# Norm statistics with tokens on partitions: root and reciprocal over 128x4 elements, spread to a bank by TensorE

## The reference

```python
def _rms_norm(x, g):
    xf = x.astype(jnp.float32)
    y = xf * lax.rsqrt(jnp.mean(xf * xf, axis=-1, keepdims=True) + NORM_EPS)
    return (y * g.astype(jnp.float32)).astype(x.dtype)

x = x + _diff_attention(_rms_norm(x, a_norm_g[j]), ...)   # blocks 0 and 3
x = x + _conformer_conv(_rms_norm(x, b_norm_g[j]), ...)   # block 1
x = x + _mla(_rms_norm(x, c_norm_g[j]), ...)              # block 2
# second network, per layer:
h = rmsnorm(x, norm1_g[layer]) * (1 + scale) + shift
x = x + g1 * mixer_or_attention(h)
x = x + g2 * swiglu(rmsnorm(x, norm2_g[layer]) * (1 + scale2) + shift2, w_gu, w_down)
```

## Time and profile before

| | us |
|---|---|
| median of 3 runs | 3501.59 (3496.18 to 3503.17) |
| profiled execution, its own time | 3498.49 |
| its span | 3496.7 |
| TensorE busy, matmuls | 3179.1 (91%) |
| TensorE busy, weight loads | 2494.1 (71%) |
| VectorE busy | 1874.4 (54%) |
| ScalarE busy | 1124.6 (32%) |
| GpSimd busy | 112.7 (3%) |

### The profile page before, as it was taken

The page is one execution under the profiler, slowest core; times in us unless marked ns, Lnnn a source line. Parts: engine busy times, 40 slices in busy tenths (PEclk is TensorE's granted clock), DMA queues, the critical chain, the costliest instruction groups (busy, mean ns, idle before and its releaser), DMA issues. The chain is left out here.

```text
span 3496.7 us, 39262 instructions
## 1 busy us (share of the span) xinstructions
PE 3179.1 (91%) x15464; PEld 2494.1 (71%) x15464; DVE 1874.4 (54%) x2778; ACT 1124.6 (32%) x2065; POOL 112.7 (3%) x114
## 2 busy tenths in 40 slices
PE   6998897899889988988999897799999989989997
PEld 4876564666668753478888566688888867767875
DVE  4648698844765677634234698524333355442333
ACT  3346323344342632232122222321211144532221
POOL 0000000100100000001000021000000000000000
PEclk9999999899999999999999998999999999999999
DMA  4224211321322241221111225312222111122221
GB/s 147 85 61 157 90 50 62 129 72 37 134 101 91 73 165 80 89 80 48 62 61 36 95 73 207 130 60 97 84 77 78 51 57 30 66 73 95 96 89 56
DMA packets 57151, 299.18 MB, mean 86 GB/s; under 512 B 8375, under 2 KB 8631, under 8 KB 31080
## 3 DMA queue, kind: packets, MB, share of 16 engines
q1 hardware_dynamic: 52504, 280.87, 22.7%
q0 software_dynamic: 4496, 16.26, 1.5%
HBM read 269.05 MB, written 15.73 MB: 81 GB/s over the span
## 5 line engine op out<-in xcount | busy, mean ns | idle before, releaser
L410 PE MATMUL bank<-high,slot_high 128*128 128x512 f32 (+1 forms) x3344 | 1236.3, 370 | 122.5 <-DVE low L334 77.8
L411 PE MATMUL bank<-low,slot_high 128*128 128x512 f32 (+1 forms) x3344 | 1226.0, 367 | 0.0
L412 PE MATMUL bank<-high,slot_low 128*128 128x512 f32 (+1 forms) x3344 | 1222.1, 365 | 0.0
L390 DVE TENSOR_TENSOR slot_low<-slot,slot_high 128x2048 fp32r<-128x2048 f32 (+1 forms) x172 | 390.3, 2270 | 1053.9 <-ACT slot_high L384 1053.8
L410 PEld LDWEIGHTS bank<-high,slot_high 128*128 128x128 f32 x3344 | 633.8, 190 | 261.1 <-issue 118.2
L384 ACT ACTIVATE slot_high<-slot 128x2048 fp32r<-128x2048 f32 (+1 forms) x172 | 325.5, 1893 | 1354.0 <-PE bank L412 1161.4
L411 PEld LDWEIGHTS bank<-low,slot_high 128*128 128x128 f32 x3344 | 635.5, 190 | 109.1 <-issue 4.6
L412 PEld LDWEIGHTS bank<-high,slot_low 128*128 128x128 f32 x3344 | 633.8, 190 | 108.0
L1089 DVE TENSOR_REDUCE least<-bank 128x1 f32<-128x128 f32 (+2 forms) x224 | 105.2, 504 | 131.5 <-PE bank L3402 51.7
L1140 ACT ACTIVATE prob<-bank,least 128x128 f32<-128x128 f32 (+2 forms) x224 | 121.2, 555 | 36.8 <-DVE least L1093 29.8
L449 PE MATMUL bank<-slot_high,low 128*128 128x256 f32 x448 | 125.7, 280 | 0.0
(11 more groups left out here) (381 smaller groups left out, 3778.0 us busy)
## 6 DMA issues: line engine op xcount, KB each, us to landing
slot<-in_gu SPq DMA_DIRECT2D x44, 1024.0 KB, 4.8
slot<-in_a_in SPq DMA_DIRECT2D x32, 1024.0 KB, 4.9
mod_raw<-in_mod SPq DMA_DIRECT2D x44, 512.0 KB, 4.7
slot<-in_e_rest SPq DMA_DIRECT2D x16, 1024.0 KB, 4.8
slot<-in_down SPq DMA_DIRECT2D x16, 1024.0 KB, 4.7
a_value<-in_mod SPq DMA_DIRECT2D x24, 512.0 KB, 3.4
spectra<-f_spectrum SPq DMA_DIRECT2D x12, 1024.0 KB, 3.8
h_spectrum<-spectra SPq DMA_DIRECT2D x12, 1024.0 KB, 5.0
```

Source lines behind the costliest of these rows:

```text
L390: dve.tensor_tensor(k.slot_low[s][:, 0:n], k.slot[s][:, 0:n], k.slot_high[s][:, 0:n].bitcast(F32), ALU.subtract).then_inc(k.low[s], 1)
L410: pe.matmul(out, wh, xh, start=kt == 0, stop=False)
L411: pe.matmul(out, wh, xl, start=False, stop=False)
L412: mm = pe.matmul(out, wl, xh, start=False, stop=kt == self.kt - 1)
```

## The change

The means come out with tokens on partitions. The squares are now the stationary operand, 128 tokens at a time, and a single column of the mean matrix is the moving one: four fp32 matmuls per 512 tokens and k tile, each with one column, and the bank holds 128x4 elements. ScalarE reads the bank and takes the root of mean plus 1e-6 (a bias column `eps`), VectorE the reciprocal, both over 128x4 (128x2 for context). TensorE then spreads it: with the column of 128 tokens broadcast as stationary operand and the identity as moving operand, four matmuls fill the bank with the reciprocals, repeated on all partitions. The feed's `make` reads the bank, and the bank is given back when all tiles are made. `take_means` and the 512-wide root and reciprocal remain for `Statistics` alone.

Beside it: a dummy root (`warm_root`) runs ahead of the squares, both in the norms that sum their own and in `TailSquares`; the feed makes two tiles ahead in the place of three, in all feeds; the second weight split always follows the feed; and in `project_a` VectorE runs the norm before it waits for the lambda vectors. The core of the diff:

```diff
 class Core:
+        self.token_root, self.token_rstd = (self.sb(n, TOK // P) for n in ("token_root", "token_rstd"))
+        self.warm, self.warmed = self.sb("warm", 16), 0
...
+    def warm_root(self, act):
+        act.activation(self.warm[:, self.warmed:self.warmed + 1], self.c("eps", 1), ACT.Sqrt)
+        self.warmed += 1
...
 class Feed:
-        for y in range(3):
+        for y in range(2):
             build(y)
...
-            build(y + 3)
+            build(y + 2)
...
 class SplitNorm:
     def make(self, y, dst):
+        rstd = self.k.rstd[:, c:c + n] if self.given else self.k.ps[7 - r][:, 0:n]
         return self.dve.scalar_tensor_tensor(dst, self.k.X[:, kt * TOK + c:kt * TOK + c + n], self.gain(r, kt),
-                                             self.k.rstd[:, c:c + n], ALU.mult, ALU.mult)
+                                             rstd, ALU.mult, ALU.mult)
...
     def square(self, k, act):
+        k.warm_root(act)
...
     def take_roots(self, k, act, u):
         for r, (c, n) in enumerate(self.ranges):
+            act.wait_ge(k.filled[7 - r], self.full(u, r))
+            act.activation(k.token_root[:, self.token_columns(r)], k.ps[7 - r][:, 0:n // P], ACT.Sqrt,
+                           bias=k.c("eps", 1)).then_inc(root.sem, 1)
...
     def tensor(self, k, pe, u):
+        if not self.summed:
...
+                mm = sum_tokens(k, pe, k.ps[7 - r], self.operand.ring[y % 4][:, 0:self.ranges[r][1]], kt == 0, kt == KT - 1)
...
+        for r, (c, n) in enumerate(self.ranges):
+            pe.wait_ge(inverse.sem, inverse.at(r + 1))
+            for j in range(n // P):
+                one = k.token_rstd[:, 4 * r + j:4 * r + j + 1]
+                mm = pe.matmul(k.ps[7 - r][:, j * P:(j + 1) * P], one.broadcast_to([P, P]), k.c("ident"),
+                               start=True, stop=True)
+            mm.then_inc(wide.sem, 1)
...
     def vector(self, k, dve, u):
+        halve_first(k, dve, u, "take_low", self.phase, 0)
+        if not self.given:
+            self.invert(k, dve)
+            dve.wait_ge(wide.sem, wide.at(len(self.ranges)))
+        self.feed.vector(k, dve)
+        if not self.given:
+            dve.wait_ge(made.sem, made.at(len(self.order)))
+            for r in range(len(self.ranges)):
+                dve.sem_inc(k.drained[7 - r], 1)
+        halve_first(k, dve, u, "take_low", self.phase, 1)
...
     def invert(self, k, dve):
+            dve.wait_ge(root.sem, root.at(r + 1))
+            dve.reciprocal(k.token_rstd[:, at], k.token_root[:, at]).then_inc(inverse.sem, 1)
...
+def sum_tokens(k, pe, bank, squares, first, last):
+    tiles = squares.shape[1] // P
+    for j in range(tiles):
+        mm = pe.matmul(bank[:, j:j + 1], squares[:, j * P:(j + 1) * P], k.c("mean", 1), start=first and j == 0,
+                       stop=last and j == tiles - 1)
+    return mm
...
 class TailSquares:
+                if f == 0:
+                    k.warm_root(act)
...
-        pe.matmul(k.ps[7][:, :], k.c("mean"), self.sum[:, :], start=True, stop=False)
+        sum_tokens(k, pe, k.ps[7], self.sum[:, :], True, False)
...
-            mm = pe.matmul(k.ps[7][:, :], k.c("mean"), self.ring[f % 4][:, 0:LAT], start=False, stop=f == 7)
+            mm = sum_tokens(k, pe, k.ps[7], self.ring[f % 4][:, 0:LAT], False, f == 7)
...
 def project_a(...):
         def _(dve):
+            norm.vector(k, dve, u[3])
             dve.wait_ge(loaded.sem, loaded.at(16))
...
-            norm.vector(k, dve, u[3])
```

More of the change, by code:

```diff
@@ L53 @@
 CON, CON_COLS = layout([("ones", P), ("mean", P), ("ident", P), ("rot64", P), ("rot128", P), ("one_row", 31 + P),
-                        ("four_rows", 12 + P), ("two_rows", 4 + P), ("inv_n", 1), ("length", 2)])
+                        ("four_rows", 12 + P), ("two_rows", 4 + P), ("inv_n", 1), ("eps", 1), ("length", 2)])
 class Signal:
@@ L626, in square, with token_columns, take_roots @@
                .then_inc(squares.sem, 1)
+    def token_columns(self, r):
+        at = 4 * r
+        return slice(at, at + self.ranges[r][1] // P)
+    def take_roots(self, k, act, u):
+        root = k.named("root_ready")
+        for r, (c, n) in enumerate(self.ranges):
+            act.wait_ge(k.filled[7 - r], self.full(u, r))
+            act.activation(k.token_root[:, self.token_columns(r)], k.ps[7 - r][:, 0:n // P], ACT.Sqrt,
+                           bias=k.c("eps", 1)).then_inc(root.sem, 1)
@@ new lines, in tensor @@
+    def tensor(self, k, pe, u):
+        if self.given:
+            return
+        if not self.summed:
+            squares, added = k.named("squares"), k.named("square_added")
+            for b in self.banks():
+                pe.wait_ge(k.drained[b], u.free(b))
+            for y, (kt, r) in enumerate(self.order):
+                pe.wait_ge(squares.sem, squares.at(y + 1))
+                mm = sum_tokens(k, pe, k.ps[7 - r], self.operand.ring[y % 4][:, 0:self.ranges[r][1]], kt == 0, kt == KT - 1)
+                if kt < KT - 1:
+                    mm.then_inc(added.sem, 1)
+                else:
+                    mm.then_inc(k.filled[7 - r], 1)
+        inverse, wide = k.named("rstd_ready"), k.named("rstd_wide")
+        for r, (c, n) in enumerate(self.ranges):
+            pe.wait_ge(inverse.sem, inverse.at(r + 1))
[4 more added lines that the diff above has]
+            mm.then_inc(wide.sem, 1)
+        u.add(self.banks())
@@ new lines, in vector @@
+    def vector(self, k, dve, u):
+        self.k, self.dve = k, dve
+        halve_first(k, dve, u, "take_low", self.phase, 0)
+        if not self.given:
+            self.invert(k, dve)
+            wide = k.named("rstd_wide")
+            dve.wait_ge(wide.sem, wide.at(len(self.ranges)))
+        self.feed.vector(k, dve)
+        if not self.given:
+            made = k.named("tile_made")
+            dve.wait_ge(made.sem, made.at(len(self.order)))
+            for r in range(len(self.ranges)):
+                dve.sem_inc(k.drained[7 - r], 1)
+        halve_first(k, dve, u, "take_low", self.phase, 1)
+        u.add(self.banks())
@@ new lines, in invert, with ready, counts @@
+    def invert(self, k, dve):
+        root, inverse = k.named("root_ready"), k.named("rstd_ready")
+        for r in range(len(self.ranges)):
+            at = self.token_columns(r)
+            dve.wait_ge(root.sem, root.at(r + 1))
+            dve.reciprocal(k.token_rstd[:, at], k.token_root[:, at]).then_inc(inverse.sem, 1)
+    def ready(self, k, pe):
+        low = k.named("tile_low")
+        return lambda kt: pe.wait_ge(low.sem, low.at((kt + 1) * len(self.ranges)))
+    def counts(self):
+        n, r = len(self.order), len(self.ranges)
+        return dict(**self.feed.counts(), **({} if self.given else dict(root_ready=r, rstd_ready=r, rstd_wide=r)),
+                    **({} if self.summed or self.given else dict(squares=n, square_added=n - r)))
@@ new lines, in sum_tokens, with __init__ @@
+def sum_tokens(k, pe, bank, squares, first, last):
[4 more added lines that the diff above has]
+    return mm
+class Statistics(SplitNorm):
+    def __init__(self, ring, ranges):
+        self.operand, self.ranges, self.summed, self.given = ring, ranges, False, False
+        self.order = [(kt, r) for kt in range(KT) for r in range(len(ranges))]
@@ L632, in take_roots @@
             act.activation(k.root[:, c:c + n], k.rstd[:, c:c + n], ACT.Sqrt).then_inc(root.sem, 1)
[L634 to L663, removed]
     def take_means(self, k, dve, u):
@@ L676, in invert @@
         dve.wait_ge(inverse.sem, inverse.at(len(self.ranges)))
[L678 to L696, removed]
     def square_some(self, k, act, steps):
@@ L3805, in constants @@
     put("inv_n", rows)
+    put("eps", np.full((P, 1), EPS))
     put("length", np.tile(np.array([[LAT, CTX]]), (P, 1)))
```

## The result

The changed kernel takes 3517.0 us (median of five runs, 3515.2 to 3520.3), the kernel before 3501.6 beside it: a ratio of 1.0043, 95% interval 1.0032 to 1.0054. It is slower by some 15 us; 3474 was forecast. The profiled execution has a span of 3513.5 us.

The account below looks back on a forecast made before the run. Projection heads, where TensorE waits for a norm and then VectorE's feed, were taken to bound it. Seven heads' gains, less 1.1 and 1.5 for other feeds, gave 27.6 us: 3474, range 3463 to 3503, likeliest alone 3465 to 3484.

Parts of the forecast that it names:

- a0: First attention's head, summing its own squares: first make 5.7 us earlier, less 0.1 for the dummy root; gain 5.3.
- f0: Head of the first feed-forward, summing its own squares: first make 6.55 us earlier, gain 5.45.
- q: Head of the last attention's projection, summing its own squares: repeats the pattern of f0, gain 5.45 us.
- twelve records at 0.11: Spread in f0 and q: with hand-overs it ends about 1.65 us after the sums.
- eight records, 0.89 us, in the place of one of 0.855: Token sums of 512 tokens in f0 and q: with the spread's four, 0.4 us more over eight k tiles.
- rival 1: TensorE's clock stays low under the token sums, 0.22 a record, costing about 28 us: 3494 to 3503; chance 0.25.
- rival 3: The table load stays on the path at four summed heads, 5.1 us: 3479; chance 0.10.
- summed heads: Conformer, latent attention, second attention and second feed-forward, squares summed in the block before: gains 2.9, 2.9, 5.0, 3.2 us.
- b: Conformer's head, squares summed in the block before: first make 2.1 us after opening, spread 1.5, gain 2.9.
- f1: Second feed-forward's head, squares summed in the block before: spread 1.05 us, first make 3.7 earlier, gain 3.2.
- lookahead: Two tiles made ahead for three, in every feed: last low half 0.3 to 1.1 us later, 6.5 in all.
- Rival 2: Pairs of load and matmul don't overlap; at 0.28 a record 65 us lost, 27.6 gained: 3539; chance 0.13.

Follow-up runs that it names:

- e1: The changed kernel with its three new small tiles in unused ends of two others, so all other tiles lie where they did before: 3507.3 us, ratio 1.0009.
- e3: As e1, but each token sum multiplies with 128 equal columns in the place of one: 3482.6 us, ratio 0.9939.
- e6: As e5, but in a0, f0 and q the dummy root with its table load comes after the fourth square: 3471.0 us, ratio 0.9905.
- e5: As e3, with three tiles made ahead again in every feed, as before the change: 3475.3 us, ratio 0.9917.
- e7: The kernel before with two tiles made ahead in the place of three, nothing else: 3506.7 us, ratio 1.0011.
- e2: The kernel before with only an unused tile of 128 bytes ahead of root, moving the tiles behind it: 3509.7 us, ratio 1.0012.
- e8: The changed kernel profiled a second time, no edit: 3516.9 us.
- e4: As e1, but the heads that sum their own squares (a0, f0, q) run the old way: 3496.9 us, ratio 0.9977.
- e10: As e6, with an unused tile of 256 bytes ahead of root: 3467.4 us, one run.
- e12: As e6, with an unused 32-byte tile at the head of conformer, latent attention, feed-forwards and last attention alone: 3465.2 us, ratio 0.9888.
- e11: As e6, with an unused tile of 32 bytes ahead of root: 3461.5 us, one run.

## Why the prediction was wrong

*The step that failed* is the pace in a0, f0 and q: "twelve records at 0.11", and with it "eight records, 0.89 us, in the place of one of 0.855". The sums ran at 0.213 a record, clock 0.50 throughout, 20.61 us in f0; a pace of 0.2 at a clock of 0.50 is the sign that the prediction itself named for rival 1. Rival 1 had this price right (14.1, 21.1 and 21.1; measured 13.78, 20.61 and 20.61) and got a chance of 0.25. The rows spoke for it: in the earlier trace rows the clock was down behind a wait, and each of these sums starts behind a wait, a0's at the kernel's start, f0's after 6.30 us. The two rows of 0.11 lie where the clock was at 1.00. (The working of the second divides by twelve where twelve loads have eleven steps, the first of them slow; the value it reached, 0.11, is that of the other ten.) e1 against e3 prices the low clock: 24.7 us by the times, 22.8 of them in the seven heads.

*A term that was missing* is that of the places, 12 us by the times and 14.1 by the pace. The change was priced by its instructions and waits; three tiles of 24, 24 and 64 bytes were not looked at. This is most of why the time lies above even rival 1's 3494 to 3503.

*A term set too low* is the table load of f0 and q, priced at nothing. The load of 1.28 stands ahead of the first square there (2211.39), where nothing covers it. e6 against e5 gives 0.7 and 2.6 us in the two heads; the 4.3 by the times is not clear of noise. In a0, "less 0.1 for the dummy root" was right, since a load stands there before and after.

*What held.* The root's load went to the tails, and rival 3 is out. The summed heads gained 3.4, 2.7, 4.8 and 2.2 for a forecast of 2.9, 2.9, 5.0 and 3.2. Their first make comes 2.64 us after the opening (377.22 - 374.58; 960.52 opened at 957.88), not 2.1: the spread takes 2.07 at the low clock, the price named for it, and not the 1.5 taken. In b the clock of 1.00 that the earlier trace rows shows was not there any more: the changed tail and the spread both ran at 0.50. In f1 the spread was priced at 1.05, for a tail that runs dense; it took 2.08, because the clock fell at the end of the tail (0.91 over its sums), and f1 gained 2.2 for 3.2. The feeds end 10.49 us after the first make in b (10.5 forecast) and 18.09 in f0 (18.1). The lookahead's 6.5 us for all feeds came out as 7.3 between e3 and e5, but as 0.7 to 7 in e7, and the heads' part of it as 1.1 for 3.85: the sign and f0's stepping held, the near hit of the sum is luck. Rival 2's 3539 needed a pace of 0.28; none came near it.

*Given back later.* With the places undone, e1 still loses 10.3 us outside the heads. Part of it is no work of the change: in the filter e2 and e7, which have the old heads, lose 3.0 and 4.8, and the changed kernel itself loses 0.7 in its first profile and 4.9 in its second (e8). So executions differ there, and that of before was a quick one. In the second attention TensorE meets a transfer that was in time before (gap 0.00) and now is not:

```profile
1205.31 0.71 PE L1270 MATMUL bank<-k_now,q_now 128*128 128x128 f32 x4 [0.53 <-DMA k_now<-a_qk]
```

The gap is 0.5 to 1.5 us in e1, e3, e5 and e6 too, 0.00 and 0.1 in e2 and e7. But it is 0.01 in e4, e10 and e12 as well, whose second attention has the changed head too and gains as much by it. So the earlier arrival alone doesn't bring on this wait; its cause stays open, as no run took the transfer apart.

*By ratios to the kernel before*: 1.0043 as changed, 1.0009 with the old places, 0.9939 with dense sums, 0.9917 with three ahead, 0.9905 with the load covered. The idea was worth about 1%, and four details of how it was put in cost 1.4%. The intervals of the first two steps stand apart; those of the third overlap a little, those of the last by half and more.

## What to carry to other kernels

Price a new TensorE step at the clock of the place where it stands: after a wait, take the low-level duration unless a row shows that work of that kind brought the clock up. When a time moves and no wait explains it, set untouched matmuls side by side and count them in a busy window: a small tile allocated early moves everything behind it. An operation put ahead to hide its cost belongs where its engine waits: in f0 and q that is behind the fourth square, and not between the opening of the block and the first. (ScalarE also idles 18.93 us just before f0 opens; a load at the end of the block ahead was not tried.)

## What was not expected of the hardware

The pace of identical, never-waiting matmuls at full granted clock changed when the tiles were moved: 2265 to 2310 in 400 us of f0, and 1.9% less time per step in f1's stretch with 32 bytes. 256 bytes gave the pace of 0 in all stages. From 1700 to 1900, where the split weights lie on the same side as the operand and moved with it, 128 bytes changed nothing: 1135 matmuls in 200 us in both kernels. The Trainium skill, "TensorE: Matmul & The Clock Gate", section "Step-by-step: what each phase is for", says that TensorE reads the moving operand and the weights through ports of their own and that loading the next weights takes no bandwidth from the running matmul. No run here takes these two reads apart. The paces show that placement is not free; what meets what was not tried.

What stays open: why f0's stretch takes one of several paces at the same displacement (0.95% above in the changed kernel twice and 0.32% below in e2 at 128 bytes; 0.95% below in e11 and 0.3% above in e12 at 32).
